# Moving the term sums and remainders at the entry of two seven-product matrix products from VectorE to GpSimd

## The reference, cut to what matters

```
# block 1
x = x + einsum("bsc,cd->bsd", mix, w_out)
h = rms_norm(x, norm_ffn)
ff = square(relu(einsum("bsd,df->bsf", h, w_ff1)))      # 1024 x 1024 x 4096
x = x + einsum("bsf,fd->bsd", ff, w_ff2)
# block 2 (hybrid_layer)
x = layer_norm(ALPHA * x + einsum("bsd,de->bse", merged, w_o), ln1_g, ln1_b)
hid = silu(x @ w_gate) * (x @ w_up)                     # 1024 x 1024 x (2 * 2816)
x = layer_norm(ALPHA * x + hid @ w_down, ln2_g, ln2_b)
```

## Time and profile before

| | us |
|---|---|
| median of 3 runs (2741.3 to 2749.03) | 2744.52 |
| the profiled execution: its own time | 2744.04 |
| its span (first to last instruction) | 2742.3 |
| PE busy in it | 2637.0 |
| DVE busy | 1640.6 |
| ACT busy | 860.3 |
| POOL busy | 361.9 |

### The profile page before, as it was taken

The page is one execution under the profiler, slowest core; times in us unless marked ns, Lnnn a source line. Parts: engine busy times, 40 slices in busy tenths (PEclk is TensorE's granted clock), DMA queues, the critical chain, the costliest instruction groups (busy, mean ns, idle before and its releaser), DMA issues. The chain is left out here.

```text
span 2742.3 us, 35649 instructions
## 1 busy us (share of the span) xinstructions
PE 2637.0 (96%) x14290; PEld 2107.8 (77%) x14290; DVE 1640.6 (60%) x2537; ACT 860.3 (31%) x1522; POOL 361.9 (13%) x191
## 2 busy tenths in 40 slices
PE   7999999999899999999999999999968999999998
PEld 5875558874488888888888888868967888887887
DVE  5894997771766655444783454323276666666446
ACT  4344454320445443211131212232143323233121
POOL 1212634420000000000011211244300000000000
PEclk9999999999899999999999999999989999999999
DMA  4011032230233337232122222252322223226131
GB/s 159 31 63 67 30 123 94 94 128 27 77 112 112 111 103 281 90 118 82 51 81 59 71 76 66 78 204 65 139 77 62 78 84 92 77 87 229 69 116 62
DMA packets 192659, 262.22 MB, mean 96 GB/s; under 512 B 15856, under 2 KB 121712, under 8 KB 192112
## 3 DMA queue, kind: packets, MB, share of 16 engines
q1 hardware_dynamic: 192496, 259.95, 28.0%
HBM read 196.80 MB, written 61.93 MB: 94 GB/s over the span
## 5 line engine op out<-in xcount | busy, mean ns | idle before, releaser
L1263 PE MATMUL ps<-gl_t,gl_slot 128*128 128x512 f32 x1056 | 242.9, 389 | 0.0
L1263 PEld LDWEIGHTS ps<-gl_t,gl_slot 128*128 128x128 f32 x1056 | 198.2, 188 | 41.2
L1263 PE MATMUL ps<-gl_b,gl_slot 128*128 128x512 f32 x768 | 182.7, 396 | 18.4 <-DVE gl_slot L3588 18.4
L1263 PE MATMUL ps<-w_hi,ff_hi 128*128 128x512 f32 x480 | 187.2, 390 | 0.0
L1263 PE MATMUL ps<-w_hi,ff_lo 128*128 128x512 f32 x480 | 186.8, 389 | 0.0
L1263 PE MATMUL ps<-w_lo,ff_hi 128*128 128x512 f32 x480 | 186.8, 389 | 0.0
L1263 PEld LDWEIGHTS ps<-gl_b,gl_slot 128*128 128x128 f32 x768 | 147.1, 192 | 50.1 <-issue 14.4
L1263 PE MATMUL ps<-ff_t,slot 128*128 128x512 f32 x768 | 179.2, 393 | 4.4 <-DVE ff_t L3029 4.4
L1263 PE MATMUL ps<-H_hi,tw_hi 128*128 128x512 f32 x448 | 175.6, 392 | 0.0
L1263 PE MATMUL ps<-H_rest,tw_hi 128*128 128x512 f32 x448 | 174.4, 389 | 0.0
L1263 PE MATMUL ps<-H_hi,tw_lo 128*128 128x512 f32 x448 | 174.3, 389 | 0.0
(11 more groups left out here) (420 smaller groups left out, 5675.9 us busy)
## 6 DMA issues: line engine op xcount, KB each, us to landing
wraw<-in_w_ff SPq DMA_DIRECT2D x32, 1024.0 KB, 5.9
ff_rows<-quad SPq DMA_DIRECT2D x64, 256.0 KB, 2.0
ff_raw<-ff_rows SPq DMA_DIRECT2D x7, 2048.0 KB, 7.9
traw<-in_w_in SPq DMA_DIRECT2D x28, 512.0 KB, 4.3
wq_raw<-in_w_in SPq DMA_DIRECT2D x6, 2048.0 KB, 8.7
wraw<-in_w_gate SPq DMA_DIRECT2D x22, 512.0 KB, 4.0
wraw<-in_w_up SPq DMA_DIRECT2D x22, 512.0 KB, 5.3
hid_rows<-gl_up SPq DMA_DIRECT2D x44, 256.0 KB, 2.0
```

The lines of the kernel that those rows point to most:

```text
L1263: mm = nc.tensor.matmul(out_ap, stationary(a, k), moving(c, k), start=(k == 0 and n == 0), stop=(k == kts - 1 and n == 2))
```

## The change

For pairs 0, 1 and 2 of both products, t4, t3 and the four remainders leave DVE and become a function on GpSimd (`pair_terms`, `gl_pair_terms`), six 128x512 subtractions with operands in SBUF alone. DVE keeps t1, t2 and the remainder of B22. On ACT the casts of t4, t3 and t2 (`round_sums`) leave the step of the pair's own row and come in the next row's step: behind that row's square and root, ahead of `round_half` of that row. Pair 3 stays on DVE and ACT in the old order. No work is added or dropped; the two plain-half results are only made in another place.

```diff
@@ ScalarE, "ff"
                 nc.scalar.copy(ff_t1[:, 0, :, cols], t1_plain).then_inc(feat_hi, 1)
+
+            def round_sums(j):
+
+                cols = slice(P * j, P * j + P)
                 act.wait_ge(sums_made, 3 * j + 2)
                 nc.scalar.copy(ff_t4[:, 0, :, cols], half_plain[j][1]).then_inc(feat_hi, 1)
                 act.wait_ge(sums_made, 3 * j + 3)
...
                 if q % 2:
+                    if q > 1:
+                        round_sums(q // 2 - 1)
                     round_half(q // 2)
                 elif q > 0:
                     round_terms(q // 2 - 1)
...
             round_terms(3)
+            round_sums(3)
@@ ScalarE, "gl"
                 if t < 4:
+                    if t > 0:
+                        gl_round_sums(t - 1)
                     gl_round_half(t)
                 else:
                     gl_round_terms(t - 4)
+                    if t == NT - 1:
+                        gl_round_sums(t - 4)
@@ GpSimd (the same again as gl_pair_terms)
+            def pair_terms(j):
+
+                hi_at = FEAT[0] + 7 * j + 2
+                cols, upper_cols = slice(P * j, P * j + P), slice(512 + P * j, 512 + P * j + P)
+                pool.wait_ge(sums_made, 3 * j + 1)
+                for h in (1, 0):
+                    G.tensor_tensor(half_plain[j][h], t2_plain, half_plain[j][h], ALU.subtract).then_inc(sums_made, 1)
+                pool.wait_ge(feat_hi, hi_at + 2)
+                G.tensor_tensor(ff_t1[:, 1, :, cols], t1_plain, ff_t1[:, 0, :, cols].bitcast(F32), ALU.subtract
+                                ).then_inc(terms_lo, 1)
+                pool.wait_ge(feat_hi, hi_at + 3)
+                pool.wait_ge(sums_made, 3 * j + 3)
+                G.tensor_tensor(ff_t4[:, 1, :, cols], half_plain[j][1], ff_t4[:, 0, :, cols].bitcast(F32), ALU.subtract
+                                ).then_inc(terms_lo, 1)
+                pool.wait_ge(feat_hi, hi_at + 4)
+                G.tensor_tensor(ff_t3[:, :, upper_cols], half_plain[j][0], ff_t3[:, :, cols].bitcast(F32), ALU.subtract
+                                ).then_inc(terms_lo, 1)
+                pool.wait_ge(feat_hi, hi_at + 5)
+                pool.wait_ge(terms_lo, 4 * j + 3)
+                G.tensor_tensor(ff_t2[:, j, 1], t2_plain, ff_t2[:, j, 0].bitcast(F32), ALU.subtract).then_inc(terms_lo, 1)
+
+            for j in range(3):
+                pair_terms(j)
@@ VectorE, "ff" (the same in "gl": last_terms is called for pair 3 alone)
+            def last_terms(j):
...
-            def rest_terms(j):
...
                     term_sums(q // 2 - 1)
                     scale_row(q)
-                    rest_terms(q // 2 - 1)
...
             term_sums(3)
-            rest_terms(3)
+            last_terms(3)
```

More of the change, by code:

```diff
@@ L2366, in gl_round_terms, with gl_round_sums @@
                 nc.scalar.copy(gl_t1[:, 0, :, cols], gl_t1_plain).then_inc(feat_hi, 1)
+            def gl_round_sums(j):
+                cols = slice(P * j, P * j + P)
                 act.wait_ge(sums_made, GL_T_SUMS + 3 * j + 2)
@@ L2570, in _, with gl_pair_terms @@
                 rest_wo(c)
+            def gl_pair_terms(j):
+                hi_at = FEAT[2] + 7 * j + 2
+                cols, upper_cols = slice(P * j, P * j + P), slice(512 + P * j, 512 + P * j + P)
+                pool.wait_ge(sums_made, GL_T_SUMS + 3 * j + 1)
+                for h in (1, 0):
+                    G.tensor_tensor(gl_half[j][h], gl_t2_plain, gl_half[j][h], ALU.subtract).then_inc(sums_made, 1)
+                pool.wait_ge(feat_hi, hi_at + 2)
+                G.tensor_tensor(gl_t1[:, 1, :, cols], gl_t1_plain, gl_t1[:, 0, :, cols].bitcast(F32), ALU.subtract
+                                ).then_inc(terms_lo, 1)
+                pool.wait_ge(feat_hi, hi_at + 3)
+                pool.wait_ge(sums_made, GL_T_SUMS + 3 * j + 3)
+                G.tensor_tensor(gl_t4[:, 1, :, cols], gl_half[j][1], gl_t4[:, 0, :, cols].bitcast(F32), ALU.subtract
+                                ).then_inc(terms_lo, 1)
+                pool.wait_ge(feat_hi, hi_at + 4)
+                G.tensor_tensor(gl_t3[:, :, upper_cols], gl_half[j][0], gl_t3[:, :, cols].bitcast(F32), ALU.subtract
+                                ).then_inc(terms_lo, 1)
+                pool.wait_ge(feat_hi, hi_at + 5)
+                pool.wait_ge(terms_lo, GL_TERMS + 4 * j + 3)
+                G.tensor_tensor(gl_t2[:, j, 1], gl_t2_plain, gl_t2[:, j, 0].bitcast(F32), ALU.subtract).then_inc(terms_lo, 1)
+            for j in range(3):
+                gl_pair_terms(j)
         @block.vector
@@ L3538, in gl_term_sums, with gl_last_terms @@
                                 gl_b22[:, :, P * j:P * j + P].bitcast(F32), sub).then_inc(drained[b], 1)
+            def gl_last_terms(j):
+                hi_at = FEAT[2] + 7 * j + 2
+                cols, upper_cols = slice(P * j, P * j + P), slice(512 + P * j, 512 + P * j + P)
                 dve.wait_ge(sums_made, GL_T_SUMS + 3 * j + 1)
@@ L3541, in gl_term_sums @@
                 V.tensor_tensor(gl_half[j][0], gl_t2_plain, gl_half[j][0], sub).then_inc(sums_made, 1)
-            def gl_rest_terms(j):
-                hi_at = FEAT[2] + 7 * j + 2
-                cols, upper_cols = slice(P * j, P * j + P), slice(512 + P * j, 512 + P * j + P)
                 dve.wait_ge(feat_hi, hi_at + 2)
@@ L3601, in gl_rest_turned @@
                     gl_term_sums(t - 4)
-                    gl_rest_terms(t - 4)
+                    if t == NT - 1:
+                        gl_last_terms(t - 4)
             def merged_drain(t, h):
```

2 lines of the change are left out of this document (removed).

## The result

The changed kernel takes 2749.86 us (median of 17 runs, 2748.68 to 2759.53) against 2743.69 us (17 runs, 2741.30 to 2749.03) in the same session: a ratio of 1.0024 [1.0017, 1.003], 6.2 us slower. The forecast was 2750.4 in a range of 2742 to 2758, with "within 0.3%" as the likeliest outcome. The profiled execution has its own time of 2749.32 us, 1.8 us above its span.

A forecast was written before the change was run, and what follows sets the result against it. PE was busy for 96% of the span, so only its waits counted, with DVE setting both beats. Own time 2744.04 + 5.4 ("ff") + 1.0 ("gl") = 2750.4 us, range 2742 to 2758.

The forecast's parts named there:

- The chain of the odd rows: "ff" odd rows: half copies wait behind ACT's t2 cast for POOL; `rest_half` 3.7 us later, turn at drain +10.9.
- The second slow clock: "ff" row 5: PE idle about 3 us as at row 3, so turn and product again take 9.5 us.
- "ff" loses 5.4 us: "ff" entry: first product comes at drain of row 7 +8.1, at 742.2 where it was 736.87.
- Even rows do not matter: "ff" even rows: POOL's first three subtractions run beside `scale_row`, which has some 3 us of slack, so no cost.
- "gl" loses 1.0 us: "gl" entry: drain of row 7 comes 1.7 us earlier, then pair 2's chain delays the first product by 2.6.
- The price of POOL: Both entries: a POOL subtraction of 128x512 from SBUF takes 1.24 us from start to start.
- POOL dearer: Rival: some 20 POOL subtractions on the chain; from 1.33 us each the loss passes 8.2 us, at 1.55 2759.5; chance 0.15.
- Hidden: Rival: half copies don't come late, PE sets the pace in "ff"; 20.5 us faster, 2723.5, or part of it; chance 0.07.
- The rule of the Trainium skill: "gl": a two-SBUF-input VectorE instruction contends with GpSimd reading SBUF, the later blocks; without it the sum would be 2747.5.

The follow-up runs named there:

- the gate: Changed kernel, but in "ff" GpSimd starts a pair only once VectorE has scaled that pair's even row; 2750.78 us, ratio 1.0025 to the kernel before.
- the one-input root: Half copies first and the gate, plus each one-row root as three steps of one tensor input; 2726.65 us, ratio 0.9934 to the kernel before.
- one tensor input: Changed kernel with three single-column two-tensor root steps rewritten as steps of one tensor and a column scalar; 2754.24 us, ratio 1.0039 to the kernel before.

## Why the prediction was right, and where its numbers were off

**How close the number is, is luck.** 2750.4 was forecast and 2749.86 measured, but the terms were off by more: "ff" lost 7.5 us in these profiles where 5.4 were forecast, and "gl" gained 1.0 where 1.0 should be lost. The two errors, +2.1 and -2.0, cancel, and 0.6 of the first and 1.0 of the second are accidents of the clock. Without these "ff" lost 6.9 us and "gl" nothing. The start of the first "ff" product at 742.14, for the 742.2 forecast, is an accident too: this execution reached the entry 1.65 us earlier than the one before. Sign and mechanism did not need the luck, as the experiments show.

**The chain of the odd rows: right.** Forecast for row 3, from its drain: `rest_half` at +7.05, turn at +10.9. Measured: 699.72 - 692.65 = +7.07 and 703.60 - 692.65 = +10.95; for row 5 the turn came at 724.25 - 713.28 = +10.97. The wait named (ACT's t2 cast, for POOL's t3 remainder) is there with 2.08 us. Taking the cast out of the way gave 9.1 us back up to `ff_t`; a remainder more on POOL cost 4.6. That is cause and size from both sides.

**The second slow clock: right.** Turn to next drain was forecast at 9.5 us for rows 3 and 5; it was 9.68 and 9.60. The one row of before was thin ground for it, as the same idle time of 2.30 us was followed by the full clock in the kernel with only "gl" changed. But with 2.85 us and more all ten odd rows of five kernels had it.

**"ff" loses 5.4 us: the term was mis-sized, it was 7.5.** The step that failed is "Even rows do not matter: ... `scale_row` has some 3 us of slack". The slack was 1.3 us: without meetings L3247 would have ended at about 690.35, 2.4 us sooner than it did, and PE's product ended at 691.65. The rows of before would have given the same 1.3 at this row: its scaling

```profile
691.91 1.28 DVE L3184 SCALAR_TENSOR_TENSOR sb<-sb 128x1024 f32<-128x1024 f32 x1
```

ends at 693.19, 1.2 us earlier without two subtractions, and PE's product ends at 693.29. Some 3 us (3.4) is the slack of row 4 alone, behind the slow product. I had looked for the meeting in "gl" alone, on 128x1024 steps, and not for the root's steps in "ff", which are 128x1 but have two tensors in SBUF too. The trace of before has such a meeting near its start, three times, on DVE and on POOL:

```profile
25.08 2.33 DVE L2593 TENSOR_TENSOR sb<-sb 128x1 f32<-128x1 f32 x1
...
25.03 2.37 POOL L2450 TENSOR_TENSOR wq_lo<-wq_raw,wq_hi 128x1024 fp32r<-128x1024 f32 x1 [6.64 <-ACT wq_hi L1903]
```

In the changed kernel they stood 0.50 + 1.03 + 0.84 = 2.4 us. 1.3 of it was slack, and PE waited the other 1.14. The drain of row 3 thus came at 8.91 from the turn of row 1, not at 693.3 - 685.39 = 7.9. That is 1.0 of the 2.1 missing; the gate gave exactly 1.0 back. 0.6 came in small parts: 0.3 in the two slow stretches, 0.2 behind the drain of row 7, 0.1 in the two chains. The last 0.6 lies between the first product and `ff_t` (13.73 us for 13.10), which starts after 7.45 us of idle time in place of 6.34 and takes 5.46 us for 5.10. It is not the edit's: with the "ff" of before, the kernel with only "gl" changed has 13.73 us there too, and the kernel with the gate has 12.57. The later even rows cost nothing: behind a slow product PE was late enough itself.

**"gl" loses 1.0 us: the sign is not borne out, it was 0.0 at the first product and -1.0 at the fourth.** The mechanism was there: L3573 took 2.07 and 2.00 us for 1.27, and POOL's own subtractions 2.25 and 2.15, each having waited for the other. But the beat was 2030.67 - 2012.88 = 17.79 us and not 18.15, so that the drain of row 7 was won by 2.6 us and not 1.7. L3578, which I had delayed by POOL, came through at 1.28; the root's steps took its meeting instead (1.04 and 1.22), at less cost. The distance from that drain to the first product was forecast at +17.6 and measured at 17.61. The -1.0 is the clock: the first product ran at the low level for 3.0 us in the changed kernel and 5.9 before, worked out from the granted clock of two windows, of which the one of after is

```profile
2066.00:2070.00 4.00, 4.00 (x12) 3.20 (x13) 0.33 (x1) 0.00 (x0) 0.00 (x0) 0.63 0.00 0
```

(before: 0.53 in 2062 to 2066, with the product begun at 2059.87). The prediction had the clock low at this product in both kernels and took its length for equal; a low stretch that is 2.9 us shorter is worth half of that. It is not the change's: two kernels with the same "gl" have the fourth product at 88.42 and 88.61, against 88.33 before. And 0.7 of it was lost again at once: the fourth product took 5.18 us, and 4.44 before. So "gl" neither lost nor gained.

**The price of POOL: right.** 1.24 us was taken; the undisturbed subtraction is 1.22 us from start to start in "ff" (695.58 to 696.80) and up to 1.26 in "gl" (2020.16 to 2021.42). The rival "POOL dearer" is out in "ff" and came true in "gl" only for the subtractions that met DVE.

**"Hidden" was the rival with the sign reversed, and its condition was well put.** It was to decide by whether the half copies come late. With them first the kernel was 7.5 us faster than before, with the gate 11.0, and with the one-input root 16.6, of 20.5 that the full cover was reckoned to give (3 x 4.39 is 13.2 and not 13.1, and in the "gl" sum 2 x 0.9 is 1.8 and not 1.7: slips of 0.1 us that change nothing).

**The rule of the Trainium skill**, "SBUF — State Buffer", "Who interferes with whom", was used with too small a reach. The trace agrees with it and adds that the size of the VectorE instruction doesn't matter: 0.16 us became up to 1.22 here, and 2.33 in the rows of before above. With the rule applied to every instruction of DVE with two SBUF tensors, the 1.0 us of the even row would have been in the sum.

## What to carry to other kernels

When work moves to a slower engine, list the queue of the third engine that hands results between them: here one ScalarE cast waited for GpSimd with four copies behind it that VectorE and TensorE needed, and it cost more than the subtractions taken off VectorE gave. Put what the critical row needs ahead of what waits for the slow engine, and start the slow engine when the fast one is in work that it can't block. Before placing GpSimd work beside VectorE, go through VectorE's list for instructions with two SBUF tensors, the tiny ones too; a form with one tensor and a column scalar passes, at 0.21 us for 0.16, which every row pays.

## What the runs showed of the hardware

- A two-tensor VectorE step on one column takes 0.16 us alone and 0.66 to 1.22 us beside GpSimd's subtraction of 128x512: it ends when that ends. The same step with one tensor and a column scalar took 0.21 us, beside it and alone. The remainders that read PSUM (L3056, L3585) kept their 0.69 us.
- The meeting works in both directions: GpSimd's 1.27 us became 2.25 behind the 128x1024 step at 2022.98. A 128x1 step that came between two of its subtractions cost GpSimd nothing that shows (2.49 us for the pair at 687.67, 1.27 behind it).
- In the "ff" entries of five kernels (the changed one, only "ff" changed, the gate alone, the t3 remainder twice, one tensor input) TensorE was idle for 2.85 to 4.62 us ahead of a turn ten times; each time it was 9.2 to 10.4 us from this turn to the next, where 7.8 is the time at the full clock. After 1.14 and 1.44 us turn and product took 1.09 and 7.03 us, the full speed. In between, the same code went both ways: 2.30 us of idle time was followed by 9.5 us in one execution and by 7.8 in another.
- In places that no edit touches, an idle time of 2.2 or 2.9 us was followed by a low clock in some executions and not in others (27.70 or 29.40 us for one product). Each such place is worth 1.3 to 2.5 us and is to be taken out before two spans are compared.
